# The leftover gate blocks of a hybrid decoder layer, issued in pieces between the small matmuls of the decode stage

## The chip, the cores and the metric

The kernel runs on one core of a Trainium2 chip. The metric is the device time of one launch in microseconds (us), lower is better. Names of engines: PE is TensorE, DVE is VectorE, ACT is ScalarE, POOL is GpSimd, SP is SyncE, which here only issues DMAs.

## The reference

One inference step of one decoder layer, in float32, for a prompt of 1024 tokens and for 8 decode sequences of 4 tokens each (32 rows). One input projection feeds three branches and, per branch, 1024 gate channels:

```
qa, ka, va, qkvb, bb, ab, zb, qc, gates = jnp.split(h @ p['w_in'], _split_points(), axis=-1)
oa = swa_fn(qa, ka, va)              # sliding-window attention with sinks
ob = _gdn_branch(qkvb, bb, ab, zb)   # gated DeltaNet with a recurrent state
oc = _mem_attend(qc, mem_k, mem_v)   # cross-attention to 256 memory rows
up = jnp.einsum('blnc,ncd->blnd', stack([oa, ob, oc]), p['w_branch'])
gate = jax.nn.sigmoid(gates.reshape(Bsz, L, N_BRANCH, D_MODEL))
mix = jnp.sum(gate * up, axis=2) @ p['w_out']
```

After it come two norms and a SwiGLU feed-forward block. In decode, each of the 8 sequences attends to its own window cache, its own memory cache (keys and values of 256 rows) and updates its own recurrent state. The change touches nothing of what is computed.

## The kernel before

All 1056 token columns (1024 prompt, 32 decode) are kept transposed in SBUF, in three chunks of 352. A product with a 128-column **panel** of `w_in` is done as 3 passes (the operands split into a high and a low part) over 8 slices of the contraction, so 24 matmuls of 352 columns for each chunk: this is a **gate block**, when the panel is one of the 24 gate panels. A panel makes three blocks, x = 3(m-16), +1, +2 for panels m = 16 to 23; block x writes PSUM bank x % 3. Panels 0 to 15 (48 blocks) are spent inside the prompt's attention stage; the 24 blocks of panels 16 to 23 are left over for the **decode stage**, whose own matmuls are small: 32 rows, or 4 to 32 columns.

A panel passes through three hands ahead of PE. SP issues the DMA of its raw weights (`load_gate`), two halves of 256 KB. POOL splits it in two instructions (L734 high part, L737 low part, which raises `w_lo`) into one of two slots. Each of the two slots is refilled only when the last block of the panel before last is done. Then PE may start block x = 3(m-16) (`wait_ge(w_lo, ...)`).

In the decode stage SP's stream is in program order, and panels 18 to 23 are loaded at fixed places among the loads of the memory caches `ck` (8 of keys, 8 of values, two buffers):

```
LOAD_G = {0: 18, 3: 19, 5: 20, 8: 21, 10: 22, 12: 23}
...
for x in range(2 * DB):
    sp.wait_ge(m_kt, 2 * x + 2)
    sp.dma_start(ck[:, x % 2], ...)
    if x in LOAD_G:
        load_gate(LOAD_G[x], ...)
```

PE raises `m_kt` by 2 when it has read a buffer of `ck`: after `mem_keys(b)` (8 transposes) and after `mem_values(b)` (8 matmuls). So the load of panel 19 is issued after `mem_keys(1)`, that of 20 after `mem_keys(3)`, 21 after `mem_keys(6)`, 22 after `mem_values(0)` and 23 after `mem_values(2)`. After its last cache load (it waits for `mem_values(5)`) SP issues the stores of the decode outputs, then the loads of the stage that follows: `brw` (the branch outputs), the branch weights, and later the gates `gat`.

ACT copies each finished gate block out of PSUM (`gates(x)`, L1612) at fixed places of its own decode stream, and PE may start block x only when block x-3 has been copied. DVE and ACT do the decode softmaxes and the DeltaNet algebra between the small matmuls; `f_dv`, `f_ac` and `f_pe` count their steps. PE's decode matmuls in order: transposes and broadcasts (up to step `bcast`), `mem_keys` and `mem_scores` for 8 sequences, `new_sc`, `win_rows`, `xt`, `u_w`, `mem_values(0)`, the state product `w_q_s` (32 matmuls, L1195), `mem_values(1)`, `vn`, `mem_values(2)`, `win_o`, `o`, `mem_values(3)`, `sumsq`, eight `update`s of the state (L1131) with `mem_values(4)` to `(7)` among them. `gate_e(x)` puts block x whole (24 matmuls) at 16 places between them. A float32 matmul appears as two records in the trace (the state product's 32 are x64); gate matmuls appear as one.

Behind the decode stage comes the branch projection (L1250): its operand `actD` is made from `brw` by ACT and DVE, in the memory that held the gate blocks' operand, and its products are multiplied with `gat` by DVE (L2180).

Of the kernel before, what the change touches and what calls it, by code (L numbers as in the profile page):

```python
# [25 lines left out]
SEQ, DB, DS = 1024, 8, 4  # L26
NS = DB * DS
N = SEQ + NS
CH = N // 3
# [60 lines left out]
def build(nc, io):  # L90
# [24 lines left out]
    wsp = sb("wsp", [P, 2, 2, KT, P], F32R)  # L115
# [692 lines left out]
    def _(pe):  # L808
# [238 lines left out]

        def gate_e(*chunks):
            for x in chunks:
                m = 16 + x // 3  # L1050
                if x % 3 == 0:
                    pe.wait_ge(w_lo, NPB + m + 3)
                gate_chunk((NPB + m) % 2, x % 3, UC + 48 + x)

        pe.sem_inc(m_kt, 4)
        pe.sem_inc(m_sc, 1)
        gate_e(0, 1, 2, 3)
        pe.wait_ge(f_in, F_IN)

        def done(mm, name):  # L1060
            mm.then_inc(f_pe, 1)

        for v in range(2):
            pe.transpose(psum[:, 5, P * v:P * v + P], lkv[:, v, :], ident)
            pe.transpose(psum[0:Dn, 5, 256 + P * v:256 + P * v + P], ext[:, v, :], ident)
        for n in range(12):
            mm = pe.transpose(psum[0:3 + NS, (3, 4, 6)[n // 4], P * (n % 4):P * (n % 4) + P], tail[:, n, :], ident)
        done(mm, "out")
        for b in range(4):
            mm = pe.transpose(psum[:, 7, P * b:P * b + P], wkv[:, 0, b, :], ident)  # L1070
        done(mm, "win_kt0")

        pe.wait_ge(f_ac, ACn("tail_out"))
        pe.wait_ge(f_dv, DVn("d3"))
        for h in range(BH):
            pe.transpose(psum[0:Dn, 3, P * h:P * h + P], dq[:, 4 + h, :], ident)
            pe.transpose(psum[0:Dn, 4, P * h:P * h + P], dq[:, 8 + h, :], ident)
        pe.matmul(psum[0:Dn, 5, 0:P], kc[0:Dn, K_D_GT:K_D_GT + NS], dug[:], start=True, stop=True)
        pe.matmul(psum[0:Dn, 5, P:2 * P], ones[0:Dn, 0:Dn], dia[:, 0], start=True, stop=True)
        pe.matmul(psum[:, 5, 2 * P:3 * P], ones[0:Dn, :], dia[:, 1], start=True, stop=True)  # L1080
        pe.matmul(psum[:, 5, 3 * P:4 * P], ones[0:Dn, :], dia[:, 2], start=True, stop=True)
        pe.matmul(psum[:, 6, 0:P], ones[0:Dn, :], dia[:, 3], start=True, stop=True)
        for h in range(BH):
            pe.matmul(psum[0:Dn, 6, P + NS * h:P + NS * h + NS], dq[:, 4 + h, :], dq[:, 4 + h, :], start=True, stop=True)
            mm = pe.matmul(psum[0:Dn, 6, 2 * P + NS * h:2 * P + NS * h + NS], dq[:, 4 + h, :], dq[:, h, :], start=True, stop=True)
# [4 lines left out]
        done(mm, "win_kt1")  # L1090
        gate_e(4)
        pe.wait_ge(f_dv, DVn("el"))
# [41 lines left out]
        for b in range(DB):  # L1134
            gate_e(5 + b)
            mem_scores(b)
            if b + 1 < DB:
                mem_keys(b + 1)
# [6 lines left out]
        for v in range(2):  # L1145
            rows = slice(64 * v, 64 * v + 64)
            bank = (4, 7)[v]
            for b in range(DB):
                pe.matmul(psum[:, bank, 0:P].rearrange("p (g b s) -> p g b s", g=4, b=DB)[:, :, b, :], wkT[rows, b, :],
                          da[rows, 0:4, DS * b:DS * b + DS], start=True, stop=True)  # L1150
            mm = pe.matmul(psum[0:Dn, bank, 256:256 + P], ext[rows, 0, :], da[rows, 0:4, :], start=True, stop=True)
        done(mm, "new_sc")
        pe.wait_ge(f_ac, ACn("mem_s"))
        for t in range(2):
            mm = pe.transpose(psum[:, 6, P * t:P * t + P], mS[:, t, :], ident)
        done(mm, "mem_rows")
        gate_e(13)
        pe.wait_ge(f_dv, DVn("at1"))
# [8 lines left out]
        done(mm, "win_rows")  # L1167
        gate_e(14)
        pe.wait_ge(f_ac, ACn("y"))
        for h in range(BH):  # L1170
            mm = pe.matmul(psum[0:Dn, 3, 2 * P + NS * h:2 * P + NS * h + NS], dyy[:, h, :], dxt[:, h, :], start=True, stop=True)
        done(mm, "xt")
        gate_e(15)
        pe.wait_ge(f_dv, DVn("mem_n"))
# [7 lines left out]
        done(mm, "u_w")  # L1182
        gate_e(16)
        pe.wait_ge(f_dv, DVn("win_n"))
# [4 lines left out]
        pe.wait_ge(f_ac, ACn("mem_p"))  # L1189
        mem_values(0)  # L1190
        pe.wait_ge(f_dv, DVn("wT"))
        pe.wait_ge(s_in, 5 + 16 * DB)
        for b in range(DB):
            for h in range(BH):
                mm = pe.matmul(psum[:, 7, 64 * h + 8 * b:64 * h + 8 * b + 8], sd[:, b, h, :],  # L1195
                               wq[:, h, b].rearrange("p a s -> p (a s)"), start=True, stop=True)
        done(mm, "w_q_s")
        mem_values(1)
        gate_e(17)
        pe.wait_ge(f_dv, DVn("vT"))  # L1200
# [3 lines left out]
        mem_values(2)  # L1204
        gate_e(18)
        pe.wait_ge(f_ac, ACn("win_p"))
# [3 lines left out]
        mm = pe.matmul(psum[:, 3, 256:512], kvo[0:Dn, 1, 1, :], sS[0:Dn, 2:4, :], start=True, stop=True)  # L1210
        done(mm, "win_o")
        pe.wait_ge(f_ac, ACn("vn"))
        pe.wait_ge(f_dv, DVn("qe"))
# [3 lines left out]
        mem_values(3)  # L1217
        gate_e(19)
        pe.wait_ge(f_ac, ACn("sq"))
# [6 lines left out]
        mem_values(4)  # L1226
        gate_e(20)
        update(3)
        mem_values(5)
        for j in range(4, 7):  # L1230
            update(j)
        mem_values(6)
        gate_e(21)
        update(7)
        done(mem_values(7), "mem_o")
        gate_e(22, 23)

# [1096 lines left out]
```

## Time and profile before

| | |
|---|---|
| device time, median of 3 runs | 2325.46 us |
| the three runs | 2317.98, 2325.46, 2333.61 us |
| span of the profiled execution, first to last instruction | 2317.8 us (the fastest of the three runs, 2317.98 us, lies 0.2 us above it) |
| PE busy | 2172.3 us, 94% of the span |
| mean granted TensorE clock | 0.957 of full |
| decode stage, from the end of its fourth gate block to the end of its last | 1019.0 to 1205.5 us of the span |

The span is what lies between the first and the last instruction of the execution that the profile shows; stretches are given in us from its start. A granted clock of 1.00 is 2.4 GHz, of 0.50 is 1.2 GHz.

### The profile page before, as it was taken

The page shows a single profiled execution, that of the slowest core. Times are in us where ns is not written, and L with a number is a line of the kernel's source. Part 1 is how long each engine was busy: PE and PEld are TensorE (multiplying, and loading weights), DVE is VectorE, ACT ScalarE, POOL GpSimd, SP SyncE. Part 2 cuts the span into 40 slices and gives each one's busy share as a digit, 9 for nine tenths or more (in the row PEclk, how much of TensorE's full clock was granted, in tenths as well). Part 3 has the DMA queues.
Part 4 walks back from the last instruction along what each step waited for, and adds up shares of the span by engine and source line. Part 5 has one row for each costly group of instructions (what it writes and reads, how often), then busy time and mean ns, then how long its engine had stood idle before and what let it go on. Part 6 is the DMA issues. An engine that isn't in the chain of part 4 may idle for free.

```text
span 2317.8 us, 36058 instructions
## 1 busy us (share of the span) xinstructions
PE 2172.3 (94%) x13799; PEld 2081.6 (90%) x13799; DVE 983.0 (42%) x1678; ACT 529.0 (23%) x1125; POOL 777.6 (34%) x340
## 2 busy tenths in 40 slices
PE   5999998799999999989989989679999999999997
PEld 4999997688888888889969989679999999999996
DVE  5554034343444434420134860554344334334336
ACT  4332152233233332321112221420000000000003
POOL 2434447222120221112123434433443443443444
PEclk9999999899999999989779999789999999999998
DMA  4323323421222221135265422321111111111113
GB/s 148 102 74 102 95 83 99 118 81 48 61 77 72 81 66 43 44 101 161 65 191 166 158 76 78 124 66 46 45 45 45 45 45 45 49 45 42 54 37 150
DMA packets 225073, 189.54 MB, mean 82 GB/s; under 512 B 24491, under 2 KB 200171, under 8 KB 224962
## 3 DMA queue, kind: packets, MB, share of 16 engines
q1 hardware_dynamic: 213074, 179.62, 25.0%
q10 hardware_dynamic: 11904, 8.52, 1.2%
q8 instruction: 75, 1.23, 0.2%
q14 instruction: 20, 0.16, 0.0%
HBM read 142.07 MB, written 47.06 MB: 82 GB/s over the span
## 4 chain that ended last, share of the span: by engine, by line
PE 86%; DVE 6%; ACT 2%; DMA 2%; issue 2%; SPq 1%; POOL 1%; DVEq 0%; ACTq 0%; POOLq 0%
PE psum L1258 22%; PE psum L830 14%; PE psum L1038 12%; PE psum L1325 10%; PE psum L908 7%; PE psum L1250 4%; PE psum L1268 4%; PE psum L1023 2%; PE psum L996 2%; PE psum L1012 1%; DMA brw<-s_br 1%; DVE xs L2213 1%; PE psum L1119 1%; PE psum L1001 1%; PE psum L840 1%
## 5 line engine op out<-in xcount | busy, mean ns | idle before, releaser
L734 POOL TENSOR_TENSOR wsp<-raw,kc 128x1024 fp32r<-128x1024 f32 x145 | 349.1, 2407 | 1434.1 <-PE psum L1038 473.8
L1258 PE MATMUL psum<-actD,wsp 128*128 128x352 f32 x3168 | 515.3, 323 | 0.9 <-DVE actD L2219 0.9
L1258 PEld LDWEIGHTS psum<-actD,wsp 128*128 128x128 f32 x3168 | 509.4, 189 | 1.0 <-DVE actD L2219 1.0
L737 POOL TENSOR_TENSOR wsp<-raw,wsp 128x1024 fp32r<-128x1024 f32 x145 | 364.1, 2511 | 11.4
L830 PE MATMUL psum<-actT,wsp 128*128 128x352 f32 (+1 forms) x1944 | 314.7, 323 | 0.0
L830 PEld LDWEIGHTS psum<-actT,wsp 128*128 128x128 f32 (+1 forms) x1944 | 306.6, 185 | 5.2
L1038 PE MATMUL psum<-actT,wsp 128*128 128x352 f32 x1728 | 304.8, 334 | 0.0
L1038 PEld LDWEIGHTS psum<-actT,wsp 128*128 128x128 f32 x1728 | 287.1, 196 | 0.1
L2268 DVE TENSOR_TENSOR accT<-accT,psum 128x352 f32<-128x352 f32 x504 | 242.3, 520 | 50.4 <-PE psum L1325 50.4
L1325 PE MATMUL psum<-fT,wsp 128*128 128x352 f32 x1512 | 250.4, 323 | 0.4 <-DVE accT L2268 0.4
L1325 PEld LDWEIGHTS psum<-fT,wsp 128*128 128x128 f32 x1512 | 244.5, 188 | 0.7 <-DVE accT L2268 0.7
L2251 DVE TENSOR_TENSOR fr<-psum,sg 128x352 f32<-128x352 f32 x66 | 34.6, 524 | 375.3 <-PE psum L1258 372.6
L1250 PE MATMUL psum<-actD,wsp 128*128 128x352 f32 x864 | 143.5, 328 | 12.2 <-DVE actD L2163 8.3
L1250 PEld LDWEIGHTS psum<-actD,wsp 128*128 128x128 f32 x864 | 141.1, 192 | 14.6 <-DVE actD L2163 5.4
L1743 ACT ACTIVATE sg<-psum 128x352 f32<-128x352 f32 x66 | 30.6, 465 | 431.0 <-PE psum L1258 431.0
L1268 PE MATMUL psum<-actD,wsp 128*128 128x352 f32 x576 | 95.8, 328 | 7.1 <-DVE actD L2190 7.1
L1268 PEld LDWEIGHTS psum<-actD,wsp 128*128 128x128 f32 x576 | 93.2, 191 | 9.8 <-issue 6.6
L1751 ACT ACTIVATE fT<-fr 128x352 fp32r<-128x352 f32 x66 | 32.9, 499 | 235.2 <-DVE fr L2251 235.2
L1575 ACT ACTIVATE pr<-psum,asm 128x256 f32<-128x256 f32 x96 | 44.7, 470 | 154.8 <-DVE asm L1980 98.9
L1970 DVE TENSOR_TENSOR xx<-xx,psum 128x512 f32<-128x512 f32 x40 | 27.5, 689 | 86.4 <-PE psum L908 86.4
L1823 DVE TENSOR_SCALAR y<-cv,scT 128x1024 f32<-128x1024 f32 (+1 forms) x24 | 35.5, 1520 | 66.4 <-ACT y L1438 58.2
L1543 ACT ACTIVATE gst<-psum 128x352 f32<-128x352 f32 x48 | 22.3, 465 | 142.7 <-PE psum L1038 142.7
(386 smaller groups left out, 2348.1 us busy)
## 6 DMA issues: line engine op xcount, KB each, us to landing
raw<-in_w_in SPq DMA_DIRECT2D x100, 256.0 KB, 4.0
raw<-in_w_ffn_in SPq DMA_DIRECT2D x88, 256.0 KB, 3.1
gat<-s_gate SPq DMA_DIRECT2D x12, 1056.0 KB, 5.1
raw<-in_w_ffn_out SPq DMA_DIRECT2D x44, 256.0 KB, 2.8
s_gate<-gst SPq DMA_DIRECT2D x48, 176.0 KB, 1.8
s_qkv<-y SPq DMA_DIRECT2D x12, 528.0 KB, 3.0
brw<-s_br SPq DMA_DIRECT2D x3, 2112.0 KB, 9.7
raw<-in_w_branch SPq DMA_DIRECT2D x24, 256.0 KB, 6.3
```

The costliest lines, as they stand in the source:

```text
L734: pool.tensor_tensor(wsp[:, slot, 0], raw[:, slot], ones.unsqueeze(1).to_broadcast([P, KT, P]), ALU.mult).then_inc(w_hi, 1)
L737: pool.tensor_tensor(wsp[:, slot, 1], raw[:, slot], wsp[:, slot, 0].bitcast(F32), ALU.subtract).then_inc(w_lo, 1)
L830: mm = pe.matmul(psum[0:m, c, 0:CH], wsp[:, slot, a, k, 0:m], actT[:, h, k, CH * c:CH * c + CH], start=(k == 0 and q == 0), stop=(k == KT ...
L908: mm = pe.matmul(psum[:, bank, w * h:w * h + w], lhs(h), rhs(h), start=True, stop=True)
L996: mm = pe.matmul(psum[:, 3, 256 * a:256 * a + 256], ain[64 * kv:64 * kv + 64, b, g + a, :], awin[64 * kv:64 * kv + 64, b, 0, :], start=Fal ...
L1023: mm = pe.matmul(psum[:, 3, w * a:w * a + w], pt[:, 2 * a + s, :], rhs, start=(s == 0), stop=(s == 1))
L1038: mm = pe.matmul(psum[:, c, 0:CH], wsp[:, slot, a, k, :], actT[:, h, k, CH * c:CH * c + CH], start=(k == 0 and q == 0), stop=(k == KT - 1 ...
L1250: mm = pe.matmul(psum[:, c, 0:CH], slab(wsp[:, :, a], n % 2)[:, k, P * half:P * half + P], actD[:, h, a4 + k, CH * c:CH * c + CH], start=( ...
L1258: mm = pe.matmul(psum[:, bank, 0:CH], wsp[:, slot, a, k, :], actD[:, h, k, CH * c:CH * c + CH], start=(k == 0 and q == 0), stop=(k == KT - ...
L1268: mm = pe.matmul(psum[:, c, 0:CH], wsp[:, slot, a, m, :], actD[:, h, (m + 4) % 8, CH * c:CH * c + CH], start=(m == 0 and q == 0), stop=(m ...
L1325: mm = pe.matmul(psum[:, 4 + x % 4, 0:CH], wsp[:, slot, a, m, :], fT[:, fs, h, CH * c:CH * c + CH], start=(q == 0), stop=(q == 2))
L2268: dve.tensor_tensor(accT[:, m, cols], accT[:, m, cols], psum[:, 4 + x % 4, 0:CH], ALU.add).then_inc(o_ad, 1)
```

## The change

The 576 matmuls of the 24 leftover blocks keep their order, their operands and their banks, but are no longer issued 24 at a time. A counter hands them out in pieces: `gate_mm(120)` first (five blocks, where four stood), then pieces of 6 to 20 between the decode matmuls, among them one of 9 after each sequence of `w_q_s` but the last, and the rest (17) at the end. The waits for the panel and for the bank stand in front of the first matmul of a panel and of a block, wherever in a piece that falls. Nothing of SP's, POOL's, ACT's or DVE's streams is changed, `LOAD_G` included.

```diff
-        def gate_e(*chunks):
-            for x in chunks:
-                m = 16 + x // 3
-                if x % 3 == 0:
+        def gate_mm(count):
+            for y in range(Gates.n, Gates.n + count):
+                x, (k, q) = y // 24, divmod(y % 24, 3)
+                m, c = 16 + x // 3, x % 3
+                a, h = ((0, 0), (0, 1), (1, 0))[q]
+                if y % 72 == 0:
                     pe.wait_ge(w_lo, NPB + m + 3)
-                gate_chunk((NPB + m) % 2, x % 3, UC + 48 + x)
+                if y % 24 == 0:
+                    pe.wait_ge(g_ev, UC + 48 + x + 1)
+                mm = pe.matmul(psum[:, c, 0:CH], wsp[:, (NPB + m) % 2, a, k, :], actT[:, h, k, CH * c:CH * c + CH],
+                               start=(y % 24 == 0), stop=(y % 24 == 23))
+                if y % 24 == 23:
+                    mm.then_inc(g_mm, 1)
+            Gates.n += count
...
-        gate_e(0, 1, 2, 3)
+        gate_mm(120)
         pe.wait_ge(f_in, F_IN)
...
         for b in range(DB):
-            gate_e(5 + b)
+            gate_mm(20)
             mem_scores(b)
             if b + 1 < DB:
                 mem_keys(b + 1)
...
         mem_values(0)
+        gate_mm(10)
         pe.wait_ge(f_dv, DVn("wT"))
         pe.wait_ge(s_in, 5 + 16 * DB)
         for b in range(DB):
             for h in range(BH):
                 mm = pe.matmul(psum[:, 7, 64 * h + 8 * b:64 * h + 8 * b + 8], sd[:, b, h, :],
                                wq[:, h, b].rearrange("p a s -> p (a s)"), start=True, stop=True)
+            if b < DB - 1:
+                gate_mm(9)
         done(mm, "w_q_s")
         mem_values(1)
-        gate_e(17)
+        gate_mm(10)
...
         mem_values(2)
-        gate_e(18)
+        gate_mm(12)
```

All pieces, by the decode step ahead of them (before and after are counts of gate matmuls issued once the piece is out):

| behind | piece | after | before, at the same point |
|---|---|---|---|
| start of the stage | 120 | 120 | 96 |
| first transposes up to `bcast` | 6, 8, 16, 8, 8 | 166 | 96 |
| `win_kt1` | 12 | 178 | 120 |
| `mem_keys(b)`, b = 0 to 7 | 8 x 20 | 338 | 312 |
| within and behind `new_sc` | 14, 6 | 358 | 312 |
| `mem_rows`, `win_rows`, `xt`, `u_w` | 4 x 14 | 414 | 408 |
| `mem_values(0)`; within `w_q_s` | 10; 7 x 9 | 487 | 408 |
| `mem_values(1)` | 10 | 497 | 432 |
| `mem_values(2)`, `win_o`, `mem_values(3)` | 12, 8, 12 | 529 | 480 |
| `mem_values(4)`, `(5)`, `(6)`, `(7)` | 12, 8, 10, 17 | 576 | 576 |

Where it matters which matmul meets which wait, this is PE's order. First, PE around `mem_keys(1)`, whose end lets SP load panel 19 (`ck` transposes are `mem_keys`, `da,ckT` is `mem_scores`); before:

```order
L1102 MATMUL psum<-kc,ck 128x128 [waits m_ka,m_in1]
L1102 MATMUL psum<-kc,ck 128x128 x3
L1102 MATMUL psum<-kc,ck 128x128 [waits m_kd]
L1102 MATMUL psum<-kc,ck 128x128 x3
L1038 MATMUL psum<-actT,wsp 128x352 [waits g_ev,w_lo]
L1038 MATMUL psum<-actT,wsp 128x352 x23
```

and with the change (its lines lie some 20 further down):

```order
L1121 MATMUL psum<-kc,ck 128x128 [waits m_ka,m_in1]
L1121 MATMUL psum<-kc,ck 128x128 x3
L1121 MATMUL psum<-kc,ck 128x128 [waits m_kd]
L1121 MATMUL psum<-kc,ck 128x128 x3
L1062 MATMUL psum<-actT,wsp 128x352 x18
L1062 MATMUL psum<-actT,wsp 128x352 [waits g_ev,w_lo]
L1062 MATMUL psum<-actT,wsp 128x352
```

The wait for `w_lo` behind `mem_keys(1)` was that for panel 18; now it is that for panel 19, 18 gate matmuls behind `mem_keys(1)`.

Second, PE from `mem_values(0)` (`mS,ck`) into `w_q_s` (`wq,sd`); before, where the next wait for a panel is the one for 22, 24 gate matmuls and `mem_values(2)` further on:

```order
L1119 MATMUL psum<-mS,ck 128x4 [waits m_in0,f_ac]
L1119 MATMUL psum<-mS,ck 128x4 x7
L1195 MATMUL psum<-wq,sd 128x8 [waits pad0,f_dv]
L1195 MATMUL psum<-wq,sd 128x8 x31
L1119 MATMUL psum<-mS,ck 128x4 [waits m_in1]
L1119 MATMUL psum<-mS,ck 128x4 x7
L1038 MATMUL psum<-actT,wsp 128x352 [waits g_ev]
L1038 MATMUL psum<-actT,wsp 128x352 x23
```

and with the change:

```order
L1138 MATMUL psum<-mS,ck 128x4 [waits m_in0,f_ac]
L1138 MATMUL psum<-mS,ck 128x4 x7
L1062 MATMUL psum<-actT,wsp 128x352 x10
L1218 MATMUL psum<-wq,sd 128x8 [waits pad0,f_dv]
L1218 MATMUL psum<-wq,sd 128x8 x3
L1062 MATMUL psum<-actT,wsp 128x352 x8
L1062 MATMUL psum<-actT,wsp 128x352 [waits g_ev,w_lo]
L1218 MATMUL psum<-wq,sd 128x8 x4
L1062 MATMUL psum<-actT,wsp 128x352 x9
L1218 MATMUL psum<-wq,sd 128x8 x4
```

The wait for panel 22 has moved from behind `mem_values(2)` to 18 gate matmuls and 4 small ones behind `mem_values(0)`.

Third, PE behind `mem_values(2)`; before, with the wait for panel 22:

```order
L1119 MATMUL psum<-mS,ck 128x4 [waits m_in0]
L1119 MATMUL psum<-mS,ck 128x4 x7
L1038 MATMUL psum<-actT,wsp 128x352 [waits g_ev,w_lo]
L1038 MATMUL psum<-actT,wsp 128x352 x23
L1208 MATMUL psum<-sS,wkv 128x8x4 [waits f_ac]
```

and with the change, where it is the wait for panel 23:

```order
L1138 MATMUL psum<-mS,ck 128x4 [waits m_in0]
L1138 MATMUL psum<-mS,ck 128x4 x7
L1062 MATMUL psum<-actT,wsp 128x352 x7
L1062 MATMUL psum<-actT,wsp 128x352 [waits g_ev,w_lo]
L1062 MATMUL psum<-actT,wsp 128x352 x4
L1233 MATMUL psum<-sS,wkv 128x8x4 [waits f_ac]
```

Before, the wait for panel 23 stood behind `mem_values(6)`; now it stands 7 gate matmuls behind `mem_values(2)`.

## Rows read from the trace of the kernel before

**Rows 1.** The page: the span, and the granted clock in 40 slices of it.

```profile
span 2317.8 us, 36058 instructions
...
PEclk9999999899999999989779999789999999999998
```

**Rows 2.** Windows of the decode stage: stretch, length, busy time by engine, then PEclk.

```profile
core 0: us, PE busy (x) PEld busy (x) DVE busy (x) ACT busy (x) POOL busy (x), PEclk, DMA share, GB/s
1021.90:1038.90 17.00, 14.97 (x73) 12.54 (x74) 5.19 (x18) 4.81 (x9) 4.69 (x2) 0.50 0.26 89
1038.90:1093.50 54.60, 54.60 (x410) 54.51 (x408) 5.53 (x8) 9.50 (x19) 14.37 (x6) 1.00 0.58 175
1093.50:1103.70 10.20, 10.20 (x43) 9.36 (x43) 0.58 (x2) 0.74 (x4) 0.00 (x0) 0.50 0.00 0
1124.20:1144.70 20.50, 20.50 (x92) 20.50 (x92) 0.87 (x8) 0.00 (x0) 4.69 (x2) 0.50 0.23 78
1155.00:1161.70 6.70, 6.70 (x29) 6.64 (x29) 5.36 (x5) 0.31 (x1) 6.62 (x2) 0.50 0.25 66
1168.60:1175.40 6.80, 6.80 (x26) 6.80 (x26) 1.33 (x3) 0.00 (x0) 0.00 (x0) 0.50 0.25 77
1178.90:1192.50 13.60, 12.65 (x37) 8.98 (x37) 3.33 (x4) 0.00 (x0) 0.00 (x0) 0.50 0.43 144
```

**Rows 3.** Timeline of PE: start, us, instruction, in brackets the idle time before.

```profile
1003.51 15.51 PE L1038 MATMUL psum<-actT,wsp 128*128 128x352 f32 x96
1022.67 0.48 PE L1064 MATMUL psum<-kc,lkv 128*128 128x128 f32 x1 [3.65 <-DMA sks<-in_attn_sink]
...
1028.46 0.39 PE L1076 MATMUL psum<-kc,dq 128*32 128x128 f32 x1 [1.26 <-ACT tlo L1604]
...
1177.18 2.09 PE L1119 MATMUL psum<-mS,ck 128*128 128x4 f32 x16
```

**Rows 4.** The chain that ended last, in order of time: start, us, what.

```profile
1034.95 5.69 PE psum L1038 x24
1040.64 0.87 PE psum L1102 x8
...
1048.00 3.82 PE psum L1038 x24
...
1090.45 1.68 PE psum L1110 x16
...
1121.89 1.68 PE psum L1119 x16
1123.57 12.95 PE psum L1195 x64
...
1146.55 1.68 PE psum L1119 x16
```

**Rows 5.** Timeline of DVE, same columns.

```profile
1033.94 0.68 DVE L2039 TENSOR_TENSOR dkb<-psum,par 32x512 f32<-32x512 f32 x1 [10.00 <-PE psum L1085]
...
1037.68 0.27 DVE L2056 COPY del_<-psum 128x128 f32<-128x128 f32 x1
...
1228.81 0.52 DVE L2180 TENSOR_TENSOR accT<-psum,gat 128x352 f32<-128x352 f32 x1 [1.38 <-PE psum L1250]
```

**Rows 6.** Timeline of SP's queue: when DMAs are issued.

```profile
1048.44 1.02 SPq L525 DMA_DIRECT2D raw<-in_w_in x2
...
1124.02 1.02 SPq L525 DMA_DIRECT2D raw<-in_w_in x2
...
1179.71 0.83 SPq L610 DMA_DIRECT2D out_win_k_sample<-in_state_win_k x1
...
1209.50 1.42 SPq L572 DMA_DIRECT2D gat<-s_gate x2
```

**Rows 7.** Timeline of POOL: the second split of panels 18, 19, 22, 23.

```profile
1028.23 2.34 POOL L737 TENSOR_TENSOR wsp<-raw,wsp 128x1024 fp32r<-128x1024 f32 x1
...
1055.95 2.40 POOL L737 TENSOR_TENSOR wsp<-raw,wsp 128x1024 fp32r<-128x1024 f32 x1
...
1131.40 2.35 POOL L737 TENSOR_TENSOR wsp<-raw,wsp 128x1024 fp32r<-128x1024 f32 x1
...
1156.25 6.44 POOL L737 TENSOR_TENSOR wsp<-raw,wsp 128x1024 fp32r<-128x1024 f32 x1
```

More of the change, by code:

```diff
@@ L1046, in _ @@
         Dn = NS
-        def gate_e(*chunks):
-            for x in chunks:
-                m = 16 + x // 3
-                if x % 3 == 0:
-                    pe.wait_ge(w_lo, NPB + m + 3)
-                gate_chunk((NPB + m) % 2, x % 3, UC + 48 + x)
+        class Gates:
+            n = 0
+        def gate_mm(count):
[4 more added lines that the diff above has]
+                if y % 72 == 0:
+                    pe.wait_ge(w_lo, NPB + m + 3)
+                if y % 24 == 0:
[5 more added lines that the diff above has]
+            Gates.n += count
         pe.sem_inc(m_kt, 4)
         pe.sem_inc(m_sc, 1)
-        gate_e(0, 1, 2, 3)
+        gate_mm(120)
         pe.wait_ge(f_in, F_IN)
@@ L1065, in _ @@
             pe.transpose(psum[0:Dn, 5, 256 + P * v:256 + P * v + P], ext[:, v, :], ident)
+        gate_mm(6)
         for n in range(12):
             mm = pe.transpose(psum[0:3 + NS, (3, 4, 6)[n // 4], P * (n % 4):P * (n % 4) + P], tail[:, n, :], ident)
+            if n == 5:
+                gate_mm(8)
         done(mm, "out")
@@ L1071, in _ @@
         done(mm, "win_kt0")
+        gate_mm(16)
         pe.wait_ge(f_ac, ACn("tail_out"))
@@ L1077, in _ @@
             pe.transpose(psum[0:Dn, 4, P * h:P * h + P], dq[:, 8 + h, :], ident)
+        gate_mm(8)
         pe.matmul(psum[0:Dn, 5, 0:P], kc[0:Dn, K_D_GT:K_D_GT + NS], dug[:], start=True, stop=True)
@@ L1082, in _ @@
         pe.matmul(psum[:, 6, 0:P], ones[0:Dn, :], dia[:, 3], start=True, stop=True)
+        gate_mm(8)
         for h in range(BH):
@@ L1090, in _ @@
         done(mm, "win_kt1")
-        gate_e(4)
+        gate_mm(12)
         pe.wait_ge(f_dv, DVn("el"))
@@ L1151, in _ @@
             mm = pe.matmul(psum[0:Dn, bank, 256:256 + P], ext[rows, 0, :], da[rows, 0:4, :], start=True, stop=True)
+            if v == 0:
+                gate_mm(14)
         done(mm, "new_sc")
+        gate_mm(6)
         pe.wait_ge(f_ac, ACn("mem_s"))
@@ L1156, in _ @@
         done(mm, "mem_rows")
-        gate_e(13)
+        gate_mm(14)
         pe.wait_ge(f_dv, DVn("at1"))
@@ L1167, in _ @@
         done(mm, "win_rows")
-        gate_e(14)
+        gate_mm(14)
         pe.wait_ge(f_ac, ACn("y"))
@@ L1172, in _ @@
         done(mm, "xt")
-        gate_e(15)
+        gate_mm(14)
         pe.wait_ge(f_dv, DVn("mem_n"))
@@ L1182, in _ @@
         done(mm, "u_w")
-        gate_e(16)
+        gate_mm(14)
         pe.wait_ge(f_dv, DVn("win_n"))
@@ L1204, in _ @@
         mem_values(2)
-        gate_e(18)
+        gate_mm(12)
         pe.wait_ge(f_ac, ACn("win_p"))
@@ L1211, in _ @@
         done(mm, "win_o")
+        gate_mm(8)
         pe.wait_ge(f_ac, ACn("vn"))
@@ L1217, in _ @@
         mem_values(3)
-        gate_e(19)
+        gate_mm(12)
         pe.wait_ge(f_ac, ACn("sq"))
@@ L1226, in _ @@
         mem_values(4)
-        gate_e(20)
+        gate_mm(12)
         update(3)
         mem_values(5)
+        gate_mm(8)
         for j in range(4, 7):
@@ L1232, in _ @@
         mem_values(6)
-        gate_e(21)
+        gate_mm(10)
         update(7)
         done(mem_values(7), "mem_o")
-        gate_e(22, 23)
+        gate_mm(576 - Gates.n)
         pe.sem_inc(o_mm, 48)
```

## The prediction

> **What bounds the kernel now.** I read first the page's row of the clock [rows 1]: TensorE is given its full clock nearly everywhere, and the lowest stretch in the middle of the span is the decode stage. There the windows [rows 2] show the reader the state that the change addresses: PE is busy all the time (20.50 of 20.50 us from 1124.2 on), yet the granted clock is 0.50, 1.2 GHz, in six stretches. What PE did before each fall was small work: four columns at a time (L1110, L1119), the state product, or nothing (3.65 us idle for the last decode load, [rows 3]). What it did before each rise was a whole gate block. From 1038.9 to 1093.5, where blocks of 24 alternate with 2.6 us of small work, the clock never falls. The chain [rows 4] runs through PE without a gap in all of it, so in this stage PE's time is the stage's time.
>
> The six stretches are 17.0 + 10.2 + 20.5 + 6.7 + 6.8 + 13.6 = 74.8 us, some 3 us of them idle; at full clock the rest would take half, so the low clock costs about 36 us here, and idle time 3.65 + 1.26 + 0.95 (13.60 less 12.65 us) = 5.9 us. About 41 us, 1.8% of the span, is all that better mixing could ever bring.
>
> **Prices.** A gate matmul at full clock is 3.82/24 = 0.16 us, at half clock 0.32. `mem_values` or `mem_scores` is 1.68 us at full clock, `mem_keys` 0.87 to 0.93, the state product 12.95 us with all but its first 0.63 us at half clock, so 6.8 at full [rows 4]. The clock comes back some 3.7 to 4 us into a gate block (begun at 1034.95 [rows 4], back at 1038.9; low until 1103.7 in the block that followed it [rows 2]), so each fall costs at least 2 us.
>
> **What the change does not move: the loads.** This decides my forecast. PE now runs up to 79 gate matmuls ahead of where it was, but a panel's load is still released by a `ck` read. The time from that read to the end of POOL's second split is, for panel 19, 1048.00 to 1055.95 + 2.40: **10.35 us** [rows 4, 6, 7]; for panel 22, 1123.57 to 1131.40 + 2.35: **10.2 us**; for panel 23, 1148.23 to 1156.25 + 6.44: 14.5 us, where the split once took 6.44 instead of 2.35 to 2.40; I take 10.4, as I expect DVE's long work to fall elsewhere now, and keep 14.5 as the upper bound. What is left to cover it: behind `mem_keys(1)` 18 gate matmuls, 2.9 us, so PE stands 7.5 us; behind `mem_values(0)` 18 gate matmuls and 4 small ones, 2.9 + 0.8, so 6.5 us; behind `mem_values(2)` 7 gate matmuls, 1.1 us, so 9.3 us (13.4 at most). Panel 18 is split at 1030.57 [rows 7], 1.5 us after PE can ask for it. Panels 20 and 21 have 50 and 62 gate matmuls plus small work in front (over 13 us) and are in time. These three standstills, 23.3 us, are new: before, no gate block ever waited for its panel. In a standstill the clock falls too, as it did in the 3.65 us one.
>
> **Stretch by stretch**, each as change against before, gate matmuls moved into or out of it at 0.16 us.
>
> A, end of the fourth block (1019.02 [rows 3]) to the first `mem_keys` (1040.64). The fifth block fills the wait for the load (3.65 us idle goes). The small work up to `bcast` was 11 us at half clock, is 5.0 at full without `win_kt1`; 46 gate matmuls, 7.4; waiting for panel 18, 1.5: `bcast` is done at 1023.0 + 13.9 = 1036.9. Then DVE's chain of 4.0 us (1033.94 to 1037.95, [rows 5]) ends last, since 12 gate matmuls are only 1.9 us: 1040.9. So **+0.3**, with 58 gate matmuls ahead. ACT's copies have no part in it: block 7 waits for that of block 4 some 0.9 us, inside those 4.0 us.
>
> B, to the end of the last `mem_scores` (1092.13). 160 instead of 192 gate matmuls: -5.1. Standstill +7.5. The clock: 2 gate matmuls, `mem_scores` and `mem_keys` at half clock cost 2.9 more, then 2.0 until it is back: +4.9. Sum **+7.3**.
>
> C, to the end of `mem_values(0)` (1123.57). 76 instead of 96: -3.2. The low stretch cost 5.1 before; with 14 gate matmuls in the middle of `new_sc` I let 2.0 of it stay (bounds 0 and 5.1): -3.1. Sum **-6.3**.
>
> D, to the end of `mem_values(2)` (1148.23). 83 instead of 24: +9.4. Standstill +6.5. The low stretch of 20.5 us, 10.2, goes, but PE comes out of the standstill at half clock and then has pieces of 9 gate matmuls with 0.8 us of small work between. No row shows whether that brings the clock back: all rises in [rows 2] came within whole blocks. Bounds: 2 us (it comes back as in a block) and 20 (never: 65 gate matmuls, 10.4, and 9.8 of small work all at half clock). I take 8.5, nearer to the quick rise, as gate work and small work alternate here at least as closely as from 1038.9 to 1093.5, where the clock held. Sum **+14.2**.
>
> E, to the end of `mem_values(5)` (1179.27 [rows 3]). 44 instead of 72: -4.5. Standstill +9.3. The two low stretches, 6.7 + 6.8, cost 6.8 before. Now the clock is low after the standstill, with pieces of 5, 8 and 12 between 2 to 4 us of small work: bounds 2 and 18.2 (37 gate matmuls, 5.9, and 12.3 of small work). I take 12, nearer to the slow end, as the small work here is what the clock fell in before (three of the six falls), and its rises needed blocks that are now cut in two. Sum **+9.9**.
>
> So `mem_values(5)` ends 0.3 + 7.3 - 6.3 + 14.2 + 9.9 = 25.4 us later.
>
> F, behind it. From here PE no longer sets the end. SP issues its stores in the instant when `mem_values(5)` is done (1179.71), and its stream of stores and loads brings `gat` 30 us later (issued 1209.50) [rows 6]; the sixth product with `gat` ends at 1229.34 [rows 5], 50.1 us after `mem_values(5)`. Before, PE's gates ended 26.2 us after it and just held `actD` up. Now the gate matmuls and the small work behind it are 13 us at full clock and 25 at half, under those 30 us either way: what was saved here, with 35 gate matmuls behind that point instead of 72, is not paid back but for the first products lying ready when `gat` comes. A product takes 1.9 us of PE; two are gained: -3.5 (bounds 0 and -4).
>
> Sum: 25.4 - 3.5 = **+22 us**. The profiled execution is 2317.8 us and the median 2325.46; the difference of 7.7 us has no place in the stage, so I add to the median: 2347.5, say **2348 us**, +1.0%.
>
> **A rule weighed.** In 1124.2 to 1144.7 PE is busy without a gap and the clock is 0.50 [rows 2], so busy time as such does not hold it. The Trainium skill ("TensorE: Matmul & The Clock Gate", "Why this matters for your kernels") says that the way to full throughput is to keep TensorE busy continuously. By that rule the low stretches D and E would end as soon as PE moves again; this is the first rival. The trace of before does not agree with it for small matmuls.
>
> **Rivals.**
> First, the clock holds wherever PE moves. Each standstill costs 2 us of clock and no more. B is -5.1 + 7.5 + 2 = +4.4, C -8.3, D 9.4 + 6.5 - 10.2 + 2 = +7.7, E -4.5 + 9.3 - 6.8 + 2 = 0; with A +4.1, with F +1: **2326 us**. For it: pieces of gate work are spread evenly. Against it: the falls at 1093.5 and 1124.2 came within 4 us of small work, and such runs remain.
> Second, the clock never comes back in D and E. D is 9.4 + 6.5 - 10.2 + 20 = 25.7, E -4.5 + 9.3 - 6.8 + 18.2 = 16.2; with A to C 1.3 it is 43, with F +40: **2365 us**. For it: no piece in D or E is as long as a block. Against it: with seven and more pieces the chance recurs.
> Third, faster: the panels are in time after all, because a slot, not the `ck` read, turns out to hold the load, or SP runs ahead. Then the first rival without 23.3 us of standstill and its 6 us of clock: 1 - 29 = -28, **2297 us**. It decides from the point where the three waits are shorter than their 10 us; the rows of SP (1048.44, 1124.02, right behind the `ck` reads) speak clearly against it.
> That the change doesn't do what it says is excluded by PE's order, which shows the pieces in place.
>
> **How the numbers follow.** Forecast 0.50 (2338 to 2358, from the bounds of D), first rival 0.22, second 0.22, third 0.06. A measurement of this kernel tells about 1%, 23 us, from no change. The forecast's centre lies at that line: half of it counts as slower by over 1%. Slower: 0.24 + 0.22 = 0.46; within 1%: 0.26 + 0.22 = 0.48; faster: 0.06. The range takes in most of both near rivals, with 2 us around the first and 3 above the second for what one run differs from another; what it leaves out is the third and some 0.12 of the tails: 2324 to 2368.
>
> **What would show it.** Idle time of PE ahead of gate matmuls released by POOL's second split, 7, 6 and 9 us, at the three places; none ahead of the first transposes. Clock 1.00 up to the first standstill, 0.50 behind each. `mem_values(5)` some 25 us later, the gate blocks ended 13 to 25 us behind it, and PE then idle until `actD` is there. I am wrong if the standstills are missing (the loads were not what I took them for), or if the clock in the state product's pieces stays at one level all through, high or low, which moves the sum by 6 us down or 18 up.

## The result and the profile after

The changed kernel takes **2357.18 us** (median of 4 runs, 2354.45 to 2358.44), against 2321.72 us for the kernel before in the same comparison (4 runs, 2316.45 to 2333.61): ratio **1.0146**, 95% interval 1.0115 to 1.0176. It is slower, by some 34 us where +22 was forecast. The medians lie 35.5 us apart. The span of the profiled execution is 2356.6 us, 38.8 more than before, of which 8.0 us lie ahead of the stage.

The page has the span and the granted clock in 40 slices, as [rows 1]. The low part in the middle is longer and deeper:

```profile
span 2356.6 us, 36058 instructions
...
PEclk7999998899999999998858999889999999999998
```

The stage begins, with its first large piece, at 1011.5 us where it began at 1003.5 before. That offset of 8.0 us lies in a part of the program that the change does not touch, and it is no effect of the change: over all profiles of this study the stage began between 1003.5 and 1015.3 us, and two controls with the stream of before, told below (e2 and e8), began it at 1005.0 and 1013.1. All stretches below are therefore counted from that start.

PE's timeline around the waits, as [rows 3] (idle time ahead of a piece in brackets; L1062 are gate matmuls, L1138 is `mem_values`):

```profile
1011.52 19.32 PE L1062 MATMUL psum<-actT,wsp 128*128 128x352 f32 x120
...
1038.95 1.59 PE L1062 MATMUL psum<-actT,wsp 128*128 128x352 f32 x6 [2.00 <-POOL wsp L737]
...
1069.32 0.95 PE L1062 MATMUL psum<-actT,wsp 128*128 128x352 f32 x2 [7.97 <-POOL wsp L737]
...
1147.12 0.66 PE L1062 MATMUL psum<-actT,wsp 128*128 128x352 f32 x1 [6.22 <-POOL wsp L737]
...
1180.57 1.83 PE L1062 MATMUL psum<-actT,wsp 128*128 128x352 f32 x5 [9.00 <-POOL wsp L737]
...
1194.66 3.87 PE L1062 MATMUL psum<-actT,wsp 128*128 128x352 f32 x12
...
1237.08 4.74 PE L1062 MATMUL psum<-actT,wsp 128*128 128x352 f32 x17
1248.44 2.37 PE L1277 MATMUL psum<-actD,wsp 128*128 128x352 f32 x6 [6.62 <-POOL wsp L737]
```

Before, no gate matmul waited for its panel. Now four do, each time for POOL's second split. The sum by the view of PE's waits (total, times, longest):

```profile
PE psum L1062 <- POOL wsp L737: 25.2, 4, 9.0
```

SP's queue shows why: the loads of panels 19, 22 and 23 are issued in the same instant as ever, right behind the `ck` reads, while PE wants the panels 18 gate matmuls or fewer after those reads ([rows 6] has the same rows of before):

```profile
1058.92 1.02 SPq L525 DMA_DIRECT2D raw<-in_w_in  x2
...
1137.47 1.02 SPq L525 DMA_DIRECT2D raw<-in_w_in  x2
...
1170.78 1.05 SPq L525 DMA_DIRECT2D raw<-in_w_in  x2
```

The windows, as [rows 2], show what each standstill leaves behind (PE's busy time, then the other engines', PEclk, DMA):

```profile
1039.60:1043.00 3.40, 3.40 (x16) 2.78 (x15) 0.00 (x0) 0.00 (x0) 0.00 (x0) 0.50 0.00 0
1063.50:1077.20 13.70, 7.88 (x34) 7.88 (x35) 0.69 (x1) 0.95 (x2) 4.67 (x2) 0.50 0.70 165
1111.40:1118.00 6.60, 6.60 (x25) 5.79 (x25) 0.00 (x0) 0.00 (x0) 0.00 (x0) 0.50 0.00 0
1118.00:1142.00 24.00, 22.90 (x166) 21.24 (x166) 4.56 (x23) 5.47 (x20) 0.00 (x0) 1.00 0.24 74
1142.00:1152.20 10.20, 5.08 (x20) 5.08 (x21) 0.00 (x0) 0.00 (x0) 4.67 (x2) 0.50 0.05 18
1152.20:1172.70 20.50, 19.37 (x145) 18.98 (x145) 3.15 (x9) 0.93 (x2) 0.00 (x0) 1.00 0.17 47
1172.80:1241.00 68.20, 60.43 (x192) 47.70 (x193) 16.12 (x23) 3.53 (x7) 4.68 (x2) 0.50 0.32 104
```

The reader is to see two things. The state product, at 0.50 nearly throughout before, now runs at 1.00 (1152.2 to 1172.7): spreading gate matmuls did do that. But from 1172.8, inside the third standstill, PE is at half clock for 68.2 us, until it is in the last piece of gate work, though it is busy for 60.4 of them and does pieces of gate work of 5, 8, 12, 12, 8 and 10 matmuls in them.

Stretch by stretch, in us from the start of the stage, read from PE's timeline (each end is where the next group of matmuls begins; E's is where `mem_values(5)` itself ends):

| end of | before | after | change of the stretch | predicted |
|---|---|---|---|---|
| A: first `mem_keys` begins | 37.0 | 40.0 | +3.1 | +0.3 |
| B: last `mem_scores` | 88.5 | 98.5 | +6.9 | +7.3 |
| C: `mem_values(0)` | 119.9 | 125.4 | -4.5 | -6.3 |
| D: `mem_values(2)` | 144.6 | 158.7 | +8.6 | +14.2 |
| E: `mem_values(5)` | 175.8 | 205.6 | +15.7 | +9.9 |
| F: sixth product with `gat` | 225.8 | 258.0 | +2.3 | -3.5 |

The changes are taken before rounding. Up to the sixth product the stage costs 32.1 us; from there to the end the two profiles differ by 1.4 us.

Each column is one execution, and the stage itself differs from one execution to the next. In the two controls with PE's order of before (and other loads or stores on SP), the sixth product came at 218.1 us (e2) and 215.8 us (e8), not at 225.8. Stretch B is firm (51.5 or 51.6 us long in all three). D was 24.7 us long before and 21.4 and 24.6 in the controls, 33.3 in the changed kernel; E was 31.2, 27.9 and 29.5 before and in the controls, 46.9 in the changed kernel. So the growth of D and E is beyond that spread, but a difference of a few us between two profiles can be this spread alone.

### The profile page after: what moved, and what is told of

The parts are those of the page before. It is cut to its first block, busy times and chain, and to the rows that moved or that the text cites. A ratio compares the mean times of both kernels' runs of the same rounds, so it can differ in the third digit from the quotient of the medians.

```text
span 2356.6 us, 36058 instructions
## 1 busy us (share of the span) xinstructions
PE 2184.4 (93%) x13799; PEld 2084.0 (88%) x13799; DVE 987.7 (42%) x1678; ACT 527.2 (22%) x1125; POOL 774.2 (33%) x340
## 4 chain that ended last, share of the span: by engine, by line
PE 84%; DVE 6%; DMA 3%; ACT 2%; issue 2%; POOL 2%; SPq 1%; DVEq 0%; ACTq 0%; POOLq 0%
PE psum L1285 22%; PE psum L830 13%; PE psum L1352 10%; PE psum L1038 8%; PE psum L908 7%; PE psum L1277 4%; PE psum L1295 4%; PE psum L1062 3%; PE psum L1023 2%; PE psum L996 2%; DMA raw<-in_w_in 1%; PE psum L1012 1%; PE psum L1138 1%; DMA brw<-s_br 1%; DVE xs L2240 1%
## 5 line engine op out<-in xcount | busy, mean ns | idle before, releaser
L1038 PE MATMUL psum<-actT,wsp 128*128 128x352 f32 x1152 | 196.1, 325 | 0.0
L1062 PE MATMUL psum<-actT,wsp 128*128 128x352 f32 x576 | 118.1, 362 | 25.9 <-POOL wsp L737 25.2
L1062 PEld LDWEIGHTS psum<-actT,wsp 128*128 128x128 f32 x576 | 105.3, 215 | 28.9 <-POOL wsp L737 26.3
```

The costliest lines, as they stand in the source:

```text
L1038: mm = pe.matmul(psum[:, c, 0:CH], wsp[:, slot, a, k, :], actT[:, h, k, CH * c:CH * c + CH], start=(k == 0 and q == 0), stop=(k == KT - 1 ...
L1062: mm = pe.matmul(psum[:, c, 0:CH], wsp[:, (NPB + m) % 2, a, k, :], actT[:, h, k, CH * c:CH * c + CH], start=(y % 24 == 0), stop=(y % 24 == ...
```

## The experiments

All ran on the same chip. Those with labels e1 to e4 share one set of runs of the kernel before (median 2319.24 us), e5 to e9 another (2321.07), e10 a third (2317.59). "Standstill" is a wait of PE for POOL's split ahead of a gate matmul.

**All loads early.** The first question is whether it is the loads or the pieces. This is the changed kernel with panels 19 to 23 each released some `ck` reads earlier, nothing else:

```diff
-    LOAD_G = {0: 18, 3: 19, 5: 20, 8: 21, 10: 22, 12: 23}
+    LOAD_G = {0: 18, 1: 19, 2: 20, 4: 21, 6: 22, 8: 23}
```

> The changed kernel with the panel loads released earlier: panel 19 goes behind the second cache load instead of the fourth, 20 behind the third, 21 the fifth, 22 the seventh, 23 the ninth. Theory L (late loads: the standstills, and the falls of the clock that they bring, are the cost): the three standstills of 8.0, 6.2 and 9.0 us go, and with them most of the 44 us in which the clock stays at 0.50 behind the third; 35 to 45 us less than the changed kernel, 2312 to 2322 us. Theory P (pieces: matmuls in pieces of 8 to 12 cannot hold the clock at full between small matmuls, whatever the loads do): only the standing time of 23 us comes back, 2334 us, and the windows behind mem_values(2) still show 0.50.

Measured: 2318.09 us, ratio 0.999 (0.9965 to 1.0014). The three standstills are gone; one wait of 2.5 us, for panel 18, stays. So the whole loss of 1.5% hangs on when the panels arrive. The other half of the answer is in the windows:

```profile
1100.30:1103.70 3.40, 3.40 (x13) 3.03 (x11) 0.00 (x0) 0.00 (x0) 0.00 (x0) 0.51 0.00 0
1103.70:1144.60 40.90, 40.90 (x293) 39.52 (x292) 5.44 (x31) 5.47 (x20) 9.47 (x4) 0.96 0.11 36
1144.60:1148.00 3.40, 3.40 (x14) 3.34 (x14) 0.00 (x0) 0.00 (x0) 0.00 (x0) 0.50 0.40 131
1148.00:1158.30 10.30, 10.30 (x78) 9.56 (x76) 4.52 (x7) 1.59 (x4) 0.00 (x0) 1.00 0.24 78
1158.30:1206.00 47.70, 47.70 (x145) 36.14 (x145) 13.88 (x18) 2.87 (x5) 0.00 (x0) 0.50 0.44 140
```

From the scores to 1158.3 the clock is low in three stretches of 3.4 us only (1100.3, 1107.1, 1144.6), and the state product is done at 1.00. From 1158.3 on it is 0.50 for 47.7 us in which PE never stands, and its work there is the tail of the stage with its pieces of 12:

```profile
1159.51 3.87 PE L1062 MATMUL psum<-actT,wsp 128*128 128x352 f32 x12
1163.17 0.63 PE L1246 MATMUL psum<-dsq,kc 128*128 128x128 f32 x2
1163.73 5.48 PE L1150 MATMUL psum<-vnm,dkd 32*128 32x512 f32 x6
1169.14 3.58 PE L1138 MATMUL psum<-mS,ck 128*128 128x4 f32 x16
1172.58 3.87 PE L1062 MATMUL psum<-actT,wsp 128*128 128x352 f32 x12
```

A piece of 12 takes 3.87 us at half clock, and some 9 us of small work follow the first of these two. Of the Trainium skill's advice to keep TensorE busy continuously ("TensorE: Matmul & The Clock Gate", "Why this matters for your kernels") the trace bears out the half on idle gaps (each of the three long waits for a panel in the changed kernel is followed by a low clock), and not the other: here PE was busy in 47.70 of 47.70 us and had half clock in all of them.

**The same loads in the kernel before**, as a control for the queue order alone.

> Control: the kernel before (whole blocks) with the same earlier loads. No block waited for its panel there, so both theories expect no change, 2316 to 2328 us, unless the earlier loads delay the cache loads, which would cost some us between mem_keys.

2321.3 us, ratio 1.0009 (0.9986 to 1.0032). Where no gate block comes early, early loads are worth nothing; e1's recovery is the standstills, not a better SP queue.

**Only panel 23 early.** One standstill alone, the third, with nothing else changed:

```diff
-    LOAD_G = {0: 18, 3: 19, 5: 20, 8: 21, 10: 22, 12: 23}
+    LOAD_G = {0: 18, 3: 19, 5: 20, 8: 21, 9: 23, 10: 22}
```

> The changed kernel with the load of panel 23 alone moved, from behind the read of mem_values(2) to ahead of panel 22's load; the first two standstills stay. Theory L: the third standstill (9.0 us) goes and the clock, which fell in it, stays at 1.00 until a later stretch of small work; 9 + 10 to 15 us less, 2332 to 2338 us. Theory P: 9 us less, 2348 us, with 0.50 from win_o on.

2336.13 us, ratio 1.0073 (1.0038 to 1.0107). The standstills of 8.0 and 6.5 us are there, the third is not:

```profile
1150.30:1177.50 27.20, 27.20 (x203) 26.47 (x203) 6.52 (x15) 2.44 (x5) 0.00 (x0) 1.00 0.17 51
...
1184.50:1218.50 34.00, 34.00 (x108) 26.25 (x108) 6.58 (x9) 0.46 (x1) 0.00 (x0) 0.50 0.49 158
```

In the profiles the sixth product comes 20.3 us sooner than in the changed kernel (237.7 for 258.0 us from the start of the stage); by the two ratios it is 17 us. So a standstill of 9.0 us cost about twice its length: the rest is the clock, which is low for 34 us at the end of the stage (and 3.4 us ahead of that) instead of 68. One thing in it speaks against a simple rule. The clock fell at 1177.6, 0.7 us into this piece of 12, and was back at 1181.0 (0.98 in the window of 1 us from there), where the same piece in e1, begun 1.2 us behind a fall, brought nothing back:

```profile
1176.97 3.34 PE L1062 MATMUL psum<-actT,wsp 128*128 128x352 f32 x12
...
1186.29 3.87 PE L1062 MATMUL psum<-actT,wsp 128*128 128x352 f32 x12
```

It was low again from 1184.5 on, through the pieces of 12, 8 and 10 that followed, until 1218.5, inside the piece of 17.

**Whole blocks from `mem_values(0)` on.** The changed kernel up to `u_w` (the last 14 there made 8, so that 408 gate matmuls are out as before), and from there the order of before, a block of 24 at a time; the loads are the original ones.

```diff
-        gate_mm(10)            # behind mem_values(0)
+        gate_mm(0)
...
-                gate_mm(9)     # seven times, within w_q_s
+                gate_mm(0)
...
-        gate_mm(10)            # behind mem_values(1)
+        gate_mm(24)
-        gate_mm(12)            # behind mem_values(2)
+        gate_mm(24)
```

> The changed kernel's pieces up to u_w (that one cut from 14 to 8), and from mem_values(0) on whole blocks where the kernel before has them; loads as before. Only the first standstill is left. If my stretch-by-stretch sum is right, stretches D and E carry 24 of the 30 us by which mem_values(5) came later, so this is 5 to 8 us above before, 2326 to 2331 us, with the clock of before behind mem_values(0). If the cost were in A to C, it would stay near 2350 us.

2326.72 us, ratio 1.004 (1.0022 to 1.0058). One standstill of 8.1 us (panel 19) and the 1.9 us for panel 18 are left, 9.9 in all, and the loss is 0.4% or 9 us. That is about as long as its standstills; by the two ratios some 25 of the 34 us were lost behind `mem_values(0)`.

**The tail held back.** With all loads early, is the low clock of the tail due to the length of its pieces? This is e1, with the pieces of 12, 12, 8 and 10 gathered into 30 behind `mem_values(5)` and 12 behind `mem_values(6)`:

```diff
-        gate_mm(12)            # behind mem_values(3)
+        gate_mm(0)
...
-        gate_mm(12)            # behind mem_values(4)
+        gate_mm(0)
...
-        gate_mm(8)             # behind mem_values(5)
+        gate_mm(30)
...
-        gate_mm(10)            # behind mem_values(6)
+        gate_mm(12)
```

> e1 with the two pieces of 12 behind mem_values(3) and (4) moved behind mem_values(5), where pieces of 30, 12 and 17 now stand. In e1 the clock was at 0.50 from mem_values(3) on and no piece of 8 to 17 brought it back. Theory S (what SP issues behind mem_values(5) sets the next stage, PE's gates there are under it): the 24 gate matmuls cost 7.7 us at half clock ahead of mem_values(5) and nothing behind it, so 6 to 8 us less than e1, 2311 us. Theory G (the end of the gate blocks sets the next stage, wherever they stand): only what the clock gains in the piece of 30, 2 to 4 us less than e1.

2310.54 us, ratio 0.9959 (0.9938 to 0.998). The windows:

```profile
1150.80:1171.00 20.20, 20.20 (x62) 14.87 (x62) 10.13 (x13) 2.17 (x4) 0.00 (x0) 0.50 0.36 122
1171.00:1177.70 6.70, 6.70 (x36) 4.75 (x34) 2.07 (x3) 0.00 (x0) 0.00 (x0) 1.00 0.43 139
```

and PE's timeline:

```profile
1166.38 7.09 PE L1062 MATMUL psum<-actT,wsp 128*128 128x352 f32 x30
...
1184.50 4.53 PE L1062 MATMUL psum<-actT,wsp 128*128 128x352 f32 x17
1198.02 3.01 PE L1277 MATMUL psum<-actD,wsp 128*128 128x352 f32 x9 [8.99 <-POOL wsp L737]
```

Without gate work the tail is low as before, but the piece of 30, begun at 1166.38, brings the clock back at 1171.0. The gate matmuls end 183 us into the stage instead of e1's 197. PE then stands 9 us for the first branch weights, which come through SP and POOL, so that of those 13.4 us 11.8 reach the start of the long run of products; at the sixth product the profiles are 14.5 us apart (207.6 for 222.1). The measured gain over e1 is smaller, 0.3%, with intervals that overlap: e5's profiled execution is the fastest of its ten.

**As many gate matmuls in the tail, but whole.** e5 changed two things, the length of pieces and how many gate matmuls lie ahead of `mem_values(5)`. This one keeps e1's count, 42 in the tail, and makes them 24 and 18:

```diff
-        gate_mm(12)            # behind mem_values(3)
+        gate_mm(24)
...
-        gate_mm(12)            # behind mem_values(4)
+        gate_mm(0)
...
-        gate_mm(8)             # behind mem_values(5)
+        gate_mm(18)
...
-        gate_mm(10)            # behind mem_values(6)
+        gate_mm(0)
```

> e1 with the same number of gate matmuls ahead of mem_values(5), but in longer pieces: 24 behind mem_values(3) instead of 12 and 12, and 18 behind mem_values(5) instead of 8 and 10. Theory P (a short piece does not bring the clock back, a long one does): the window of the piece of 24 shows the clock back at 1.00 some 4 us into it, it falls again in the updates, so 3 to 6 us less than e1, 2313 us. If the length does not matter, as e1.

2309.79 us, ratio 0.9958 (0.9933 to 0.9983). In the timeline and the windows the piece of 24 begins at 1155.96, the clock falls at 1156.3 and is back within the piece, at 1159.6:

```profile
1155.96 5.63 PE L1062 MATMUL psum<-actT,wsp 128*128 128x352 f32 x24
```

```profile
1156.30:1159.60 3.30, 3.30 (x13) 3.30 (x12) 2.59 (x1) 0.63 (x1) 0.00 (x0) 0.50 0.57 196
1159.60:1166.50 6.90, 6.90 (x38) 5.03 (x36) 4.25 (x10) 1.12 (x3) 0.00 (x0) 0.99 0.14 52
```

From `mem_values(2)` to `mem_values(5)` the same work, 24 gate matmuls behind `mem_values(3)` and `(4)` included, takes 24.7 us here and 31.8 in e1. At an equal count the whole piece did better in these two executions. That the cutting made all of e1's 47.7 low us isn't shown: by the measured times the gain over e1 is 0.3%, and the intervals of the two ratios just overlap.

**Stores early.** e5 stood 9 us for SP's queue. In e7 the stores of the window and convolution outputs, ready long before, are issued within SP's cache loads instead of behind them:

```diff
         for x in range(2 * DB):
...
+            if x == 9:
+                for v, (src, dst, pdst) in enumerate((("state_win_k", "win_k_sample", "win_k_prompt"), ("state_win_v", "win_v_sample", "win_v_prompt"))):
...
+                sp.wait_ge(f_ac, ACn("tail_out"))
+                sp.dma_start(io["conv_prompt"][0], tlo[0:3, :]).then_inc(f_st, 16)
...
-        for v, (src, dst, pdst) in enumerate((("state_win_k", "win_k_sample", "win_k_prompt"), ("state_win_v", "win_v_sample", "win_v_prompt"))):
...
-        sp.wait_ge(f_ac, ACn("tail_out"))
-        sp.dma_start(io["conv_prompt"][0], tlo[0:3, :]).then_inc(f_st, 16)
```

> e5 with SP's stores of the window and convolution outputs (11 us of issuing behind mem_values(5)) issued with the tenth cache load. Theory S: the loads of brw, branch weights and gat come 11 us earlier, and the next stage starts up to 8 us earlier, until the end of the gate blocks holds it; 2303 us. Theory G: as e5, within 2 us.

2306.4 us, ratio 0.9938 (0.9919 to 0.9958). 2303 us was expected if SP's queue sets the next stage, e5's time within 2 us if the gates do; the result lies between. The wait of 9 us for POOL is a shorter one for `actD`, made by DVE:

```profile
1214.78 1.22 PE L1278 MATMUL psum<-actD,wsp 128*128 128x352 f32 x3 [3.76 <-DVE actD L2191]
```

The long run of products begins 7.0 us behind the last gate matmul instead of 13.4, but from `mem_values(5)` to the sixth product it is only 2.2 us less (44.7 for 46.9). Against e5 the measured gain is 0.2%, within the two intervals.

The profiled execution is the slowest of its seven (2321.73 us), and it limits what the profiles above show. PE's order is that of e5, yet its clock was low for 44 us (a window of the stage, columns as before):

```profile
1149.00:1193.20 44.20, 44.20 (x156) 37.37 (x156) 15.27 (x19) 4.00 (x8) 0.00 (x0) 0.50 0.23 74
```

It fell in `mem_values(1)`, and the pieces of 10, 12 and 8 that in e5 ran at full clock until 1150.4 were done at half; only the piece of 30 brought it back. Only SP's stores lie elsewhere than in e5, and e10 below, with the same stores, kept the clock through those pieces of 12 and 8. So the same order on PE can keep or lose the clock from one execution to another, and one profile alone doesn't prove what a tail's pieces do.

The same stores moved in the kernel before, with the early loads:

> The kernel before (whole blocks) with the earlier panel loads of e2 and the earlier stores of e7. There the gate blocks end 26 us behind mem_values(5) and actD is made only after them. Theory S: some 2 to 4 us less than e2, as gat and the weights then wait for nothing, 2317 us. Theory G: as e2.

2316.86 us, ratio 0.998 (0.9963 to 0.9997). There the gain is 0.2%, barely clear of nothing. A reason that fits, not tested apart: in this kernel PE's own gate blocks end about as late as SP's queue does.

**All together.** This is e9 with e7's stores, and with matmuls traded between the two pieces around panel 18's wait so that the panel is asked for later (behind the first transposes 16 and 8 become 10 and 14).

> All that helped in one kernel: panel loads early (e1), 24 behind mem_values(3) instead of 12 and 12 and 18 behind mem_values(5) (e9), SP's stores early (e7), and the first matmul of panel 18 later: the pieces of 16 and 8 around the first dq transposes become 10 and 14. If the gains add up (e9's 0.4%, e7's 0.2% against e5, 1 us of the 2 us wait for panel 18): 0.993 of before, 2304 us. If the early stores only show where the tail was held back as in e5, as e9, 0.996.

2303.86 us against 2317.59, ratio **0.994** (0.9927 to 0.9953), 0.6% faster than the kernel before and 53 us faster than the changed one by the medians. By the ratios it can't be told from e7 (0.9938) or e9 (0.9958). The waits of PE for POOL in the stage:

```profile
PE psum L1063 <- POOL wsp L738: 0.2, 1, 0.2
```

With panel 18 in time the clock stays at 1.00 from the start of the stage into `new_sc`:

```profile
1012.70:1098.70 86.00, 84.42 (x614) 81.97 (x613) 11.30 (x27) 15.78 (x33) 23.16 (x10) 1.00 0.66 194
```

## Why the prediction was right, and where its terms were off

The sign, the range (2324 to 2368) and the mechanism held: the standstills are at the three places named, and each is followed by half clock. The sum was 10 to 14 us short, made of terms that missed in both directions. That it came so near is in part luck: the clock terms of D and E missed by 5 us one way and 6 us the other, and cancel.

**The loads.** 7.5, 6.5 and 9.3 us were predicted, 7.97, 6.22 and 9.00 measured. Panel 18 took 2.00 for 1.5. This is the step on which the forecast rested, and e1 with its control e2 shows it as cause: moved loads, no loss. The third rival (panels in time) falls with the rows of the result.

**A, +0.3 against +3.1.** The clock was assumed to be 1.00 until the first standstill. It is 0.50 from 1039.6 to 1043.0, right behind the wait for panel 18. The wait of 2 us and the low stretch together fit the miss. e10 bears it out: with a wait of 0.2 us there is no low stretch here, and the first `mem_keys` begins at 36.8 us instead of 40.0. All seven profiles of cut orders with a wait for the panel, 1.9 to 2.5 us, had a low stretch there. (e10 also traded six matmuls between two pieces, so the wait wasn't varied quite alone.)

**B, +7.3 against +6.9.** Right in its total and nearly in its parts.

**C, -6.3 against -4.5.** Of the cost of the low stretch in `new_sc`, 5.1 us before, the prediction let 2.0 stay. The stretch was 6.6 us long at half clock, so 3.3 us of cost.

**D, +14.2 against +8.6.** The clock term was set at 8.5, between 2 and 20. With the measured standstill it comes out as 8.6 - 9.4 - 6.2 + 10.2 = 3.2. The clock was back at 1152.2, 5.1 us after PE moved again: pieces of 9 with small work of 0.8 us at full clock between them did about as well as blocks. The first rival's view was right here.

**E, +9.9 against +15.7.** The same working gives 15.7 + 4.5 - 9.0 + 6.8 = 18.0 for the clock, where 12 was taken and 18.2 was the bound for a clock that never returns. It never did within E. The reasoning that pieces of 5 to 12 between long small work would not raise it was right for this execution; the value was drawn toward the middle without a row for a middle. This is the term that failed most, and it is the second rival's. e3 shows how it hangs together with the standstill: take away 9.0 us of waiting and about 20 us go.

**F, -3.5 against +2.3.** The prediction said that PE no longer sets the end behind `mem_values(5)`. But its 35 gate matmuls and small work at half clock ended 24.7 us behind that point, hardly sooner than before (26.2), and `actD` can only be made when they are done, as it takes the memory of their operand. From the last gate matmul to the long run of products it was then 14.4 us instead of 10.7: DVE's four instructions for `actD` spread over 12.2 us (9.7 before),

```profile
1243.97 12.19 DVE L2190 TENSOR_TENSOR actD<-brw,actD 128x1056 fp32r<-128x1056 f32 x4 [6.42 <-ACT actD L1699]
```

and PE's first product waited 6.62 us for POOL. So both PE and SP's chain came last, a few us apart. e5 (9 us of idle time for SP's and POOL's work once the gates ended early) shows SP's chain as a bound; how much moving it is worth beyond that the times of e7 don't tell apart from nothing.

**Readings of the rows.** The prediction reads that the clock comes back 3.7 to 4 us into a gate block, and takes 2 us as the least cost of a fall. By [rows 2] laid on PE's timeline of before, the six rises came 2.9 to 6.0 us into the block (the longest in the block begun at 1169.35, back by 1175.4), and later runs had low stretches of 3.4 us, 1.7 us of cost. Two sums are a little off: low clock and idle time make 42 us, not 41, and E's terms add up to 10.0, not 9.9.

**Where the expected gain went.** Spreading the gate matmuls could at best win back the 36 us of low clock that the prediction counted. e1 is the change without the three standstills: it holds the clock through the scores and the state product, but loses it in its tail, where the three low stretches of before, 27.1 us in all, became one of 47.7 us. Its `mem_values(5)` ends at 171.8 us, 4.0 us sooner than in the profile of before, yet 5.6 later than in that of e2, which has the same loads and whole blocks; by the medians e1 is 3 us faster than e2, with intervals that overlap. With the tail's pieces whole (e9), the gain over the kernel before is 0.4%, and with SP's stores out of the way and panel 18 in time (e10) 0.6%.

**Open.** The sum of the stage's terms is 32.1 us and the medians say 35.5, the ratio 34 (27 to 41); nothing more can be told apart at this size. Which part of e10's gain is from its stores and which from the traded pieces wasn't measured apart. And why a short piece brings the clock back in some cases isn't settled. In the stretches behind `mem_values(0)` a piece of 12 did so in e3, e5 (begun at 1178.23, back at 1181.1) and e7 (1199.99, 1203.4), and a piece of 10 in e1 (1145.01, 1148.0) and e10 (1143.61, 1146.6); in these five the clock fell between 0.7 us after the start of the piece and 0.5 us ahead of it. Where it had fallen 0.8 us or more ahead of the piece (e7's 10 at 1149.70, e1's 12 at 1159.51, e3's second 12, all those of the changed kernel's tail), it stayed low. No run varied that alone.

## What to carry to other kernels

When matmuls are moved ahead on PE, look up what releases the load of their operand: if it is a point of PE's own stream, the load must move with them, or PE stands for what its own work doesn't cover of the way from release to operand (here some 10 us, of which 6.2 to 9.0 stood open). Where the small work between two pieces was 0.8 us long, as in the state product, pieces of 9 large matmuls kept the clock at 1.00; in the tail, with 2 to 9 us of small work between pieces of 8 to 12, it was at 0.50 for 47.7 us in e1, and every piece of 17 or more that met half clock there brought it back. So there the longer pieces are the safer choice, at a gain that is small here (0.3%, not clear of the spread). And before shortening a stage, see what starts the next one: here PE stood 9 us for weights behind SP's stores once its own work ended sooner.

## What the runs showed of the hardware that was not expected

- PE was busy without a gap for 47.7 us at half clock (e1), with pieces of 12, 12, 8 and 10 gate matmuls and the greater part of a piece of 17 in it. In the tails of the cut orders every piece of 17, 18, 24 or 30 that met half clock brought it back, 2.9 to 5.4 us after its start (e3 and e10); in the changed kernel's state product the clock was back 5.1 us after the standstill, through pieces of 1 and 9 with 1.7 us of small work between.
- The same order of PE's instructions was at half clock for 20.5 us in one execution (e5, 1150.4 to 1170.9) and for 44 us in another (e7), in stretches that both end in the piece of 30.
- One standstill of 9.0 us cost 17 to 20 us (e3 against the changed kernel): about half of it came later, as low clock.
- An untouched part of the program ahead of the stage took between 1003.5 and 1015.3 us in eleven profiles, so that two profiles must be laid on one another at a landmark, not at zero.
